# A hybrid encoder layer on one core: where the blocks of modulation sums stand, and how they are turned into columns

## The reference

```python
c_act = jax.nn.silu(c)
mod = c_act @ ada_w[l] + ada_b[l]            # 1024 -> 6144
sh1, sc1, gt1, sh2, sc2, gt2 = split(mod, 6)
h = rms_norm(x, norm1_g[l]) * (1.0 + sc1) + sh1
proj = h @ w_in[l]
q, k, v, g_out, gk_low, z, xbc, dt_raw, gates = split_cols(proj, IN_SIZES)
gk = log_sigmoid(gk_low @ w_gk2 + b_gk) / 16        # in gla_mixer, then cumulated in chunks of 64
xbc = silu(causal_depthwise_conv(xbc, conv_w, conv_b))       # in ssd_mixer; 4096 channels, 4 taps
dt = softplus(dt_raw + dt_bias); d_a = -dt * exp(a_log)      # also cumulated in chunks
merged = gate_a * (o_a @ w_oa[l]) + gate_b * (o_b @ w_ob[l])
x = x + gt1 * (merged @ w_out[l])
h = rms_norm(x, norm2_g[l]) * (1.0 + sc2) + sh2
x = x + gt2 * hier_moe(h, ...)               # 32 experts, top 2 of one group
```

## Time and profile before

| | us |
|---|---|
| median of 3 runs | 741.28 (739.49 to 741.56) |
| the profiled execution | 742.72 |
| its span, first to last instruction | 740.9 |
| TensorE busy | 705.9 |
| VectorE busy | 400.8 |
| ScalarE busy | 265.3 |
| mean granted clock of TensorE | 0.986 of full speed |

### The profile page before, as it was taken

The page is one execution under the profiler, slowest core; times in us unless marked ns, Lnnn a source line. Parts: engine busy times, 40 slices in busy tenths (PEclk is TensorE's granted clock), DMA queues, the critical chain, the costliest instruction groups (busy, mean ns, idle before and its releaser), DMA issues.

```text
span 740.9 us, 13185 instructions
## 1 busy us (share of the span) xinstructions
PE 705.9 (95%) x5600; PEld 570.0 (77%) x5600; DVE 400.8 (54%) x691; ACT 265.3 (36%) x375; POOL 66.6 (9%) x66
## 2 busy tenths in 40 slices
PE   9899999999999999999999999999999999997892
PEld 7689999989777777799998999886566666655541
DVE  3386778764675556997877456463423122121226
ACT  3245545547446244343635334222131122121001
POOL 0010000000000170440000000001111111111110
PEclk9998999999999999999999999999999999999997
DMA  9964647655776535334354447988999999999971
GB/s 367 416 220 178 236 169 284 229 187 220 256 281 228 192 118 173 132 126 136 113 196 148 171 168 270 423 341 313 407 416 418 418 421 420 420 419 420 420 296 58
DMA packets 30893, 200.48 MB, mean 271 GB/s; under 512 B 4999, under 2 KB 5383, under 8 KB 7410
## 3 DMA queue, kind: packets, MB, share of 16 engines
q1 hardware_dynamic: 27506, 193.01, 67.6%
q0 software_dynamic: 3328, 6.62, 2.4%
HBM read 194.57 MB, written 10.75 MB: 277 GB/s over the span
## 4 chain that ended last, share of the span: by engine, by line
PE 79%; DMA 11%; DVE 5%; ACT 2%; issue 2%; SPq 1%; DVEq 0%; ACTq 0%
PE ps L1446 77%; DMA ring<-in_expert_pieces 7%; DMA r_btm<-in_pieces 2%; DVE ring_rounded L858 1%; DMA ring<-in_pieces 1%; ACT ring_rounded L567 1%; PE ps L1566 1%; PE ps L1859 1%; SPq L422 1%; DVE r_kq L1067 0%; DVE r_xs_rounded L1130 0%; DVE x_sb L1402 0%; DVE x_sb L1429 0%; DVE x_sb L1421 0%; DVE r_kq L1061 0%
## 5 line engine op out<-in xcount | busy, mean ns | idle before, releaser
L858 DVE TENSOR_TENSOR ring_rounded<-ring,ring_rounded 128x2048 fp32r<-128x2048 f32 x60 | 138.0, 2304 | 91.4 <-ACT ring_rounded L567 91.2
L1446 PE MATMUL ps<-hT_rounded,ring_rounded 128*128 128x256 f32 x832 | 157.0, 289 | 0.9 <-DVE x_sb_rounded L897 0.9
L567 ACT CAST ring_rounded<-ring 128x2048 fp32r<-128x2048 f32 x60 | 114.2, 1904 | 70.2 <-DMA ring<-in_pieces 40.6
L1446 PEld LDWEIGHTS ps<-hT_rounded,ring_rounded 128*128 128x128 f32 x832 | 133.7, 196 | 4.1 <-issue 3.9
L1446 PE MATMUL ps<-x_sb_rounded,ring_rounded 128*128 128x256 f32 x416 | 119.4, 287 | 0.0
L1446 PE MATMUL ps<-ring_rounded,hT_rounded 128*128 128x512 f32 x352 | 109.5, 392 | 0.0
L1446 PEld LDWEIGHTS ps<-x_sb_rounded,ring_rounded 128*128 128x128 f32 x416 | 81.6, 196 | 0.2 <-issue 0.2
L1446 PEld LDWEIGHTS ps<-ring_rounded,hT_rounded 128*128 128x128 f32 x352 | 65.3, 188 | 14.9 <-issue 1.7
L1446 PE MATMUL ps<-ring,r_lm 128*64 128x256 f32 x512 | 65.4, 380 | 3.1 <-DMA ring<-in_expert_pieces 3.1
L1446 PEld LDWEIGHTS ps<-ring,r_lm 128*64 128x64 f32 x512 | 42.8, 137 | 27.1 <-issue 12.3
L788 ACT ACTIVATE sq<-ps 128x128 f32<-128x128 f32 x32 | 8.9, 277 | 147.9 <-PE ps L1446 147.9
(11 more groups left out here) (308 smaller groups left out, 1125.3 us busy)
## 6 DMA issues: line engine op xcount, KB each, us to landing
ring<-in_pieces SPq DMA_DIRECT2D x76, 1024.0 KB, 5.0
ring<-in_expert_pieces SPq DMA_DIRECT2D x48, 1024.0 KB, 20.2
r_z<-in_expert_pieces SPq DMA_DIRECT2D x12, 1024.0 KB, 16.2
r_xs<-in_expert_pieces SPq DMA_DIRECT2D x12, 1024.0 KB, 17.3
g_sb<-in_expert_pieces SPq DMA_DIRECT2D x6, 1024.0 KB, 17.9
r_st<-in_expert_pieces SPq DMA_DIRECT2D x6, 1024.0 KB, 19.0
r_bt<-in_expert_pieces SPq DMA_DIRECT2D x6, 1024.0 KB, 23.1
hT<-in_expert_pieces SPq DMA_DIRECT2D x6, 1024.0 KB, 22.6
```

What stands on the lines that cost most here:

```text
L567: nc.scalar.copy(high_of(p_), slot_of(p_)).then_inc(hi_ok, 1)
L858: nc.vector.tensor_tensor(low_of(p_), slot_of(p_), high_of(p_).bitcast(F32), ALU.subtract).then_inc(lo_ok, 1)
L1446: return nc.tensor.matmul(o, l, r, start=start, stop=stop)
```

## The change

- Modulation blocks 4 to 11 stand after xbc 0 to 7, one after each.
- Their columns are packed on the host in another order, so that a block's 512 sums come out whole in four strips of 128 columns: 32 products of 128 columns take the place of 16 of 256. Each half of a block needs one piece and is multiplied by itself when that piece is there. VectorE transposes the bank in 32x32 squares and adds the bias from there; ScalarE's copy and the four turning products are gone.
- The small projections of gk and dt are one product of 48 columns; gk comes out token-major and is transposed by TensorE (`gkT`) after xbc 3.
- The dA sums (`acum`) take both halves of the tokens in one product and stand after xbc 3, the gate products (`gklin`) after xbc 5, and VectorE copies them behind convolution halves 8 and 12. The gate chain runs once for both halves, with 1024 columns.
- The calls of `before` change with them: `before("acum")` on both engines is gone, and the one at `gsuf` now stands behind the gate chain.
- At the start the parts are issued in another order, with other fillers.

```diff
-ADA_AFTER = {("xbc", 2): 4, ("xbc", 4): 5, ("xbc", 6): 6, ("k", 0): 7, ("q", 0): 8, ("v", 0): 9, ("v", 1): 10,
-             ("g", 0): 11}
+ADA_AFTER = {("xbc", i): 4 + i for i in range(8)}
...
-PLAN += [(n, b) for b in ADA_FIRST for n in ("ada", "adc")]
+PLAN += [("ada", b) for b in ADA_FIRST]
 for _i in range(8):
     PLAN += [("unit", "xbc", _i)] + ["small"] * (_i == 0)
     if 1 <= _i <= 6:
         PLAN += [("tr", _i - 1, 0), ("tr", _i - 1, 1)]
-    if ("xbc", _i - 1) in ADA_AFTER:
-        PLAN += [("adc", ADA_AFTER["xbc", _i - 1])]
+    PLAN += {3: ["gkT", "acum"], 5: [("gklin", 0), ("gklin", 1)]}.get(_i, [])
...
+PLAN += [("unit", "k", 0)]
+PLAN += [("unit", "q", 0), ("gsuf", 0), ("gsuf", 1), "gdec"]
...
-            ada_out(7)
-            for t in range(TT):
-                act.wait_ge(gk_in, t + 1)
-                link(nc.scalar.activation(gk_abs, gk_abs, ACT.Exp, scale=-1.0))
-                nc.scalar.activation(gk_sp, gk_abs, ACT.Ln, bias=1.0).then_inc(gk_l, 1)
-            before("acum")
+            act.wait_ge(gk_in, 1)
+            link(nc.scalar.activation(gk_abs, gk_abs, ACT.Exp, scale=-1.0))
             mix_taken(act, "acum")
             nc.scalar.activation(dend, dend, ACT.Exp)
             nc.scalar.activation(eacum, acum, ACT.Exp)
             nc.scalar.activation(cdec[:], cdec[:], ACT.Exp).then_inc(eac_done, 1)
+            nc.scalar.activation(gk_abs, gk_abs, ACT.Ln, bias=1.0).then_inc(gk_l, 1)
...
             def modulation_out(i):
                 if i >= 4:
-                    before(("adc", i))
-                bank = mix_wait(dve, ("adc", i))
-                nc.vector.scalar_tensor_tensor(mod[:, 4 * i:4 * i + 4], bank[:, 0:4], 1.0 / 32, col("ada_b", 4 * i, 4), ALU.mult,
-                                               ALU.add).then_inc(mix_used(("adc", i)), 1)
+                    split_to(PIECES_OF["ada", i])
+                bank = mix_wait(dve, ("ada", i))
+                turned_ = ada_turned[:, i % 2]
+                nc.vector.transpose(turned_.rearrange("p m c -> p (m c)"), bank[:, 0:P]).then_inc(mix_used(("ada", i)), 1)
+                mix_taken(dve, ("ada", i))
+                link(nc.vector.tensor_tensor(mod[:, 4 * i:4 * i + 4], turned_[:, :, 0], col("ada_b", 4 * i, 4), ALU.add))
...
-                if g % 2 == 0 and ("xbc", g // 2 - 2) in ADA_AFTER:
-                    modulation_out(ADA_AFTER["xbc", g // 2 - 2])
-            modulation_out(6)
-
-            before("acum")
-            bank = mix_wait(dve, "acum")
-            nc.vector.tensor_copy(acum, bank[:, 0:64].rearrange("p (t h) -> p t h", t=TT))
-            nc.vector.tensor_copy(dend, bank[:, 64:128].rearrange("p (t h) -> p t h", t=TT))
-            nc.vector.tensor_copy(cdec[:].rearrange("p c h -> p (c h)"), bank[:, 128:256]).then_inc(mix_used("acum"), 1)
+                if g == 8:
+                    before("gkT")
+                    bank = mix_wait(dve, "gkT")
+                    dve.wait_ge(ones_done, 1)
+                    nc.vector.tensor_copy(gkT[0:RANK, :], bank[0:RANK, 0:T]).then_inc(mix_used("gkT"), 1)
+                    bank = mix_wait(dve, "acum")
+                    nc.vector.tensor_copy(acum, bank[:, 0:64].rearrange("p (t h) -> p t h", t=TT))
+                    nc.vector.tensor_copy(dend, bank[:, 64:128].rearrange("p (t h) -> p t h", t=TT))
+                    nc.vector.tensor_copy(cdec[:].rearrange("p (t a) h -> p a t h", a=2), bank[:, 128:256].rearrange(
+                        "p (a t h) -> p a t h", a=2, t=TT)).then_inc(mix_used("acum"), 1)
+                if g == 12:
+                    for t in range(TT):
+                        before(("gklin", t))
+                        bank = mix_wait(dve, ("gklin", t))
+                        ins = nc.vector.tensor_copy(gk_ls[:, t], bank[:])
+                        ins.then_inc(mix_used(("gklin", t)), 1)
+                if g % 2 == 0 and ("xbc", g // 2 - 1) in ADA_AFTER:
+                    modulation_out(ADA_AFTER["xbc", g // 2 - 1])
+
+            modulation_out(11)
             mix_taken(dve, "acum")
+            for t in range(TT):
+                mix_taken(dve, ("gklin", t))
             dve.wait_ge(s_const, 16)
-
             dve.wait_ge(rows_zeroed, 16 * ZERO_PARTS)
-            for t in range(TT):
-                before(("gklin", t))
-                bank = mix_wait(dve, ("gklin", t))
-                nc.vector.tensor_copy(gk_ls[:, t], bank[:]).then_inc(mix_used(("gklin", t)), 1)
-                mix_taken(dve, ("gklin", t))
-                nc.vector.scalar_tensor_tensor(gk_abs, gk_ls[:, t], -1.0, gk_ls[:, t], ALU.mult, ALU.max).then_inc(gk_in, 1)
-                dve.wait_ge(gk_l, t + 1)
-                nc.vector.scalar_tensor_tensor(gk_ls[:, t], gk_ls[:, t], 0.0, gk_sp, ALU.min, ALU.subtract
-                                               ).then_inc(gk_done, 1)
-            modulation_out(7)
-            for t in range(TT):
+            nc.vector.scalar_tensor_tensor(gk_abs, gk_ls, -1.0, gk_ls, ALU.mult, ALU.max).then_inc(gk_in, 1)
+            dve.wait_ge(gk_l, 1)
+            nc.vector.scalar_tensor_tensor(gk_ls, gk_ls, 0.0, gk_abs, ALU.min, ALU.subtract).then_inc(gk_done, 1)
+            for t in range(TT):
+                before(("gsuf", t))
                 mix_taken(dve, ("gsuf", t))
-                before((("k", 0), t))
                 unit_taken(dve, ("k", 0), t)
                 nc.vector.tensor_tensor(k_tm[:, t], k_tm[:, t], gsuf_e, ALU.mult).then_inc(kdec_done, 1)
...
-            def modulation(i, *then_keep):
-
-                bank = begin(("ada", i))
-                for h in range(2):
+            def modulation(i, halves=(0, 1)):
+
+                for h in halves:
+                    bank = mix(("ada", i))[0] if h else begin(("ada", i))
                     p_ = ("ada", i, h, 0)
                     loaded(pe, p_)
-                    for k in range(KD):
-                        j = k % 4 * 32
-                        ins = mm(bank[j:j + 32, h * HC:(h + 1) * HC], c_wide[:, k], slot_of(p_)[:, k], k < 4, k >= 4)
+                    rows_ = slot_of(p_).rearrange("p a b -> p (a b)").rearrange("p (k n) -> p k n", n=CW)
+                    for k in range(KD // 2):
+                        for j in range(4):
+                            ins = mm(bank[32 * j:32 * j + 32, 0:P], c_wide[:, h * KD // 2 + k], rows_[:, k, j * P:(j + 1) * P],
+                                     h == 0 and k == 0, h == 1 and k == KD // 2 - 1)
                     ins.then_inc(full(("ada", i)) if h else ada_read, 1)
-                    keep_clock(then_keep[h] if then_keep else 0)
-
-            def modulation_columns(i):
-
-                mix_taken(pe, ("ada", i))
-                bank = begin(("adc", i))
-                for m in range(4):
-                    ins = mm(bank[:, m:m + 1], ada_sum[:, ADA_ORDER.index(i) % 2, m * P:(m + 1) * P], ones[:, 0:1])
-                ins.then_inc(full(("adc", i)), 1)
...
-            modulation(ADA_FIRST[0], 6, 2)
-            modulation_columns(ADA_FIRST[0])
-            keep_clock(2)
-            modulation(ADA_FIRST[1], 8, 0)
-            modulation_columns(ADA_FIRST[1])
+            modulation(ADA_FIRST[0])
+            keep_clock(4)
+            modulation(ADA_FIRST[1], (0,))
+            keep_clock(32)
+            modulation(ADA_FIRST[1], (1,))
+            keep_clock(6)
+            modulation(ADA_FIRST[2], (0,))
             keep_clock(8)
-            first_half_of_first_unit()
-            modulation(ADA_FIRST[2])
-            modulation_columns(ADA_FIRST[2])
-            modulation(ADA_FIRST[3], 2, 0)
-            modulation_columns(ADA_FIRST[3])
-            keep_clock(12)
+            modulation(ADA_FIRST[2], (1,))
+            first_half_of_first_unit(0)
+            modulation(ADA_FIRST[3], (0,))
+            first_half_of_first_unit(1)
+            modulation(ADA_FIRST[3], (1,))
+            keep_clock(16)
             for i in range(8):
                 project(("xbc", i))
                 if i == 0:
 
                     pe.wait_ge(s_small, 32)
                     bank = begin("small")
-                    for k in range(KD):
-                        mm(bank[0:RANK, 0:T], wsm[:, k, 0:RANK], h_f[:, k], k == 0, k == KD - 1)
+                    n_sm = RANK + SH
                     for t in range(TT):
                         for k in range(KD):
-                            ins = mm(bank[:, T + t * SH:T + (t + 1) * SH], h_f[:, k, t * P:(t + 1) * P], wsm[:, k, RANK:], k == 0,
-                                     k == KD - 1)
+                            ins = mm(bank[:, t * n_sm:(t + 1) * n_sm], h_f[:, k, t * P:(t + 1) * P], wsm[:, k], k == 0, k == KD - 1)
                     ins.then_inc(full("small"), 1)
...
+                if i == 3:
+                    pe.wait_ge(gk_tm_ok, 1)
+                    bank = begin("gkT")
+                    for t in range(TT):
+                        ins = nc.tensor.transpose(bank[0:RANK, t * P:(t + 1) * P], gk_tm[:, t], ident)
```

(83 more changed lines are left out.)

20 lines of the change are left out of this document (4 added, 16 removed).

## The result

| | before | changed |
|---|---|---|
| median of the comparison's runs, us | 740.58 (4 runs) | 756.75 (4 runs, 755.11 to 759.9) |
| span of the profiled execution | 740.9 | 755.5 |
| mean granted clock | 0.986 | 0.974 |
| start of v, after q and the gate sums | 189.4 | 217.6 |

What follows compares the result with a forecast made beforehand. TensorE, busy 95% of the span, bounds the kernel, and VectorE's queue can stop it. Later v +15.8, savings after v -12.4, clock +4.0 give +7.4 on 741.3: 748.7, stated as 748.5 us, range 736.5 to 756.

Steps and rivals of the forecast that it cites:

- The parts: TensorE's new pieces: block 2.1 us, small projections 4.0, dA sums 1.0 saved, transposition 0.3, first unit's second half at 38.3.
- The rival of dear blocks: Modulation blocks cost 3.9 us each, eight of twelve where no wait absorbs them: 763 us, chance 0.06.
- q: Before q: its first piece is queued behind the gate chain, so TensorE stands idle 9.6 us; q starts at 189.9.
- The rival of a covered q: q's piece is ready in time, so its wait goes: 736.7 us, chance 0.07.
- Bank waits: Ends of units 3 to 6: TensorE waits 3.8, 3.1, 1.6 and 3.4 us for VectorE to free banks, together 12.
- T + 4.5: T is a convolution unit's start; landing before about this decides for no bank waits, 736.7 us, chance 0.10.
- T + 4.9: Rival of no bank waits: next piece lands by then, as single transfers do; 736.7 us, chance 0.10.
- After v: After v starts: turning products 3.8, three blocks 5.8 and waits 2.8 are gone, 12.4 us saved.
- 0.5 for a late SiLU: Term in the sum for units 1 to 7, which were to take 116.1 us and end at 169.3.
- I add 4 us: Lower granted clock: 2.4 us for q's start and 1.6 for one drop elsewhere.
- the forecast of 205.2: Start of v after q 11.5 and gate sums 3.8, 15.8 us later than 189.4, before the clock term.
- the rows on narrow stretches: Earlier trace: clock drops followed 7 and 5.8 us of narrow products; five such stretches of 5.7 to 8 us expected.

Runs made afterwards that it cites:

- the first experiment: Changed kernel with one call added, so VectorE makes q's low parts before its wait for the gate chain: 744.22 us, ratio 1.0049.
- the clock held: Changed kernel with nothing moved, only fillers put in TensorE's standstills in units 1, 3, 4, 6 and before q: 750.74 us, ratio 1.0125.
- the kernel with the zeros elsewhere: Changed kernel with q's parts early, bank copies first on VectorE and ScalarE, zeros taken from `g_sb` and written after k: 727.95 us, ratio 0.981.

## Why the prediction was right, and where it was not

The mechanisms were those forecast, and the steps that set them stand:

- **The parts.** Block 1.96 us (forecast 2.1), small projections 3.67 (4.0), start at 38.11 (38.3), transposition 0.31 (0.3), dA sums at full speed 1.0. The rival of dear blocks is out: 31 ns a record, 61 a product.
- **q.** 9.60 us (forecast 9.6), each row as in the sum; the first experiment, which takes away this place alone, gives 12.5 (11.8 in the profiles) with the low clock behind it, for 12.0. The rival of a covered q falls.
- **Bank waits.** 3.3, 3.3, none and 3.7 us for 3.8, 3.1, 1.6 and 3.4: 10.3 for 12.0. Released by the operations named. The wait in unit 5 came in other profiles (1.60 with q's parts early, 1.64 with the clock held). That single waits come this near is in part luck, as their spread from profile to profile shows. That the next piece lands after T + 4.5, and not by itself at T + 4.9, is in the chain: 7.75 to 9.24 us from issue. What I had missed is how many queues hold a bank: with VectorE's copies first, ScalarE's are the next, late by nearly the same.
- **After v.** 13.6 us back, for 12.4.

**The step that failed is two terms of the sum, both mis-sized.** First, "0.5 for a late SiLU": it is 4.30 us in unit 1. I had taken the third of three transfers to land 8.6 us on, from a stretch in which SyncE alone moves data. At this place GpSimd's zeros are moving too, which I had not counted against the change: the third transfer is issued at 52.44 to 53.00 (SyncE's row) and its cast starts at 63.95, 11.6 us after the unit's start. ScalarE in order of time:

```profile
63.95 1.90 ACT L566 CAST ring_rounded<-ring 128x2048 fp32r<-128x2048 f32 x1 [6.54 <-DMA ring<-in_pieces]
65.75 0.58 ACT L604 COPY r_lm<-ps 128x512 f32<-128x512 f32 x1
66.35 1.28 ACT L590 ACT_TABLE_LOAD   x1
67.64 0.63 ACT L590 ACTIVATE r_lm<-r_lm 128x512 f32<-128x512 f32 x1
```

The cast stands ahead of the SiLU in ScalarE's queue, and the transposes need the SiLU. The experiment with late zeros ties the wait to them: 0.2 us without. The later landing makes 3.0 of the 4.3. The other 1.3 my own landing would have given: from the cast's start to the SiLU's end are 4.3 us, of which 1.28 are a table load, so a landing 8.6 us after the unit's start has the SiLU ready at 12.9, and the unit ends at 11.6. The 0.5 stood in the sum without such a working.

Second, "I add 4 us" for the clock. The pieces at half speed are four blocks (2.60, 3.42, 3.07 and 3.64 us for 1.96 each: 4.9), transposes and dA sums (2.3), units 5 and 7 (0.5 and 0.6) and q (13.2 for 11.5: 1.7), together 10.0. The term had 2.4 for q and 1.6 for one drop elsewhere, and elsewhere they came to 8.3. I had expected that most drops hide in waits; the drop outlasts the wait and falls on the block behind it, which is needed by nothing but stands ahead of the next unit.

The account at the start of v, in us against the forecast of 205.2 + 4.0 for the clock: unit 1 starts earlier -0.9; late SiLU +3.8; bank waits -1.7; a short wait for SiLU in unit 3 +0.6; clock +6.0; cheaper blocks -1.0; units 1 to 7 at 11.6 us each, where I had 11.5, +0.8; the rest +0.8, which I haven't divided. Sum 8.4, as 217.6 - 209.2. With 1.2 more gained after v, 7.2 are left, the span's 14.6 against 7.4.

**What lowers the clock.** The Trainium skill, "TensorE: Matmul & The Clock Gate", Part 1, has an idle TensorE fall to 1.2 GHz, and I had set the rows on narrow stretches beside it. In the profile of the changed kernel the windows agree with the page: two narrow stretches without a standstill (from 46.83 and from 140.66, about 5 us each) stay at 1.00, and the clock falls behind all five standstills of 3.3 to 9.6 us. But both drops of the earlier trace rows came without a standstill, and so did the one at 50 to 54 in the kernel with the zeros elsewhere, at a place where the changed kernel, and this same kernel with 16 fillers, stayed at 1.00 (48 to 52). Nor does the length of a standstill decide by itself: with q's parts early the block behind a wait of 1.60 us takes 3.64, and with 16 fillers alone the blocks behind waits of 2.8 and 2.4 take 1.95. So idle time is not the only thing that lowers the clock; what else does, no run here isolates.

## What to carry to other kernels

A bank is freed by an in-order queue, so when work is put between two units, ask for each of the banks it takes which instruction frees it, what stands ahead of that in its queue, and when that comes; then put the copies that free banks ahead of the work for pieces still in flight, on every engine that has any. A helper that brings work up to date by an order list must be called ahead of each long wait, since moving the list's names moves the calls (here one line, 12.5 us). And price a standstill with the slow products behind it: here 10.0 us of slow products came with 24.2 us of standstills in five places. Last, read the granted clock of every run beside its time before an edit gets the credit: with fewer fillers two kernels here gained three times and twice what the start moved, and in the profiles fewer slow products make 1.7 and 3.3 us of it.

## What the runs showed of the hardware

- The granted clock stood at 0.50 to 0.57 (1.2 GHz for most or all of a window of 4 us) behind standstills of 3.3, 3.65, 4.3 and 9.6 us (0.55 from 160 to 164), and fillers in these standstills kept it at 1.00 in the windows from 68, 104 and 196 and gave 6.0 us. It also stood at 0.59 from 50 to 54 in the kernel with the zeros elsewhere, with no standstill ahead.
- A transfer of 1 MB issued singly landed in 4.87 us; the third of three took 7.75 to 9.24 us in the chain of the changed kernel. With 2 MB of zeros being written it took 10.9 (53.00 to 63.95), and at the same place with the zeros late 6.7 (52.77 to the cast at 59.44).
- A product of 128 columns in one of four strips of 32 partitions took 61 ns (64 records in 1.96 us). In 121 ns the old form did 256 columns, so the narrower products cost the same per column.
- Exp and Ln tables loaded in 1.28 us and the next activation began 0.01 us later (194.94 + 1.28 = 196.22, then 196.23). The Trainium skill, "ScalarE: Activation LUTs", What ACT_TABLE_LOAD costs, adds a drain of 1.38 us to each load; this trace again doesn't show one.
